# Hybrid layer on one core: the recurrent part's keys turned by TensorE instead of stored twice, the second norm's weights spread by TensorE instead of loaded

## The reference, cut to what matters

```python
h = rms_norm(x, norm1_w); proj = h @ w_in
# 8 heads of stick-breaking attention (width 64), 4 heads of gated delta net (width 128)
gq, gk, gv = split(silu(causal_conv(gdn_qkv)));  gq, gk = l2_normalize(gq) * 128**-0.5, l2_normalize(gk)
x = x + concat(rms_norm(attention), rms_norm(gated_delta_net(gq, gk, gv, ...)) * gate) @ w_out
x = x + peer_ffn(rms_norm(x, norm2_w))
# peer_ffn: per token 8 heads x 16 experts of 16384, chosen by top-k over sums of two key scores;
#   act = gelu(u_table[expert] . xb) * gate;  out = sum(act * v_table[expert])
```

## Time and profile before

| | |
|---|---|
| median of 3 runs | 3555.86 us (3548.87 to 3561.72) |
| the profiled execution, its own time | 3561.24 us |
| its span, first to last instruction | 3559.5 us |
| busy: PE, DVE, POOL, ACT | 66%, 65%, 65%, 24% |
| bytes moved | 1276.24 MB, mean 359 GB/s |
| of these the gathers (software queue) | 1073.87 MB |

### The profile page before, as it was taken

How to read it: one execution, slowest core, us unless ns; L and a number is a source line. 1 busy time by engine, 2 the same in 40 slices (tenths; PEclk the granted TensorE clock), 3 DMA queues, 4 the chain that set the end, 5 groups by cost and what they waited for, 6 DMA issues and landing times.

```text
span 3559.5 us, 46354 instructions
## 1 busy us (share of the span) xinstructions
PE 2354.7 (66%) x16193; PEld 1425.5 (40%) x16193; DVE 2318.2 (65%) x5421; ACT 849.8 (24%) x2344; POOL 2308.0 (65%) x2091
## 2 busy tenths in 40 slices
PE   7663546885847759767848859758847784344477
PEld 6543424653524436534524536534514451000011
DVE  3436887776697597666698587667696658444400
ACT  3330012331213223313114123314103311111122
POOL 1001775555667777677777677577687768777775
PEclk9887657897868879878869879878858885555555
DMA  7542899998989999999999999999999999999999
GB/s 233 190 169 97 312 356 328 351 374 301 349 321 357 410 373 411 412 381 390 409 374 387 409 384 410 368 389 395 406 371 369 407 409 346 387 409 409 409 403 374
DMA packets 398905, 1276.24 MB, mean 359 GB/s; under 512 B 44302, under 2 KB 99667, under 8 KB 389459
## 3 DMA queue, kind: packets, MB, share of 16 engines
q0 software_dynamic: 294912, 1073.87, 78.2%
q1 hardware_dynamic: 85330, 157.45, 12.2%
q10 hardware_dynamic: 18432, 41.95, 3.2%
HBM read 1232.18 MB, written 40.93 MB: 358 GB/s over the span
## 4 chain that ended last, share of the span: by engine, by line
POOL 25%; PE 24%; DVE 18%; DMA 17%; issue 9%; ACT 3%; DVEq 3%; ACTq 1%; SPq 0%; POOLq 0%
PE zz L1489 14%; POOL u_ring L684 13%; POOL v_ring L699 11%; DMA v_ring<-in_peer_v,idxT 9%; DVE u_ring L1067 5%; PE va L1489 4%; PE rr L1489 4%; DMA u_ring<-in_peer_u,idx 4%; DMA u_ring<-in_peer_v,idxT 2%; PE ox L1489 1%; DMA work<-d_w 1%; POOL u_ring L699 1%; DVE work L1398 1%; DVE work L1400 1%; DMA work<-d_gv 1%
## 5 line engine op out<-in xcount | busy, mean ns | idle before, releaser
L684 POOL DMA_INDIRECT u_ring<-in_peer_u,idx x1024 | 1177.2, 1150 | 786.4 <-DVE work L1414 330.3
L1067 DVE SCALAR_TENSOR_TENSOR u_ring<-u_ring,hn_t 128x1024 f32<-128x1024 f32 x1024 | 1223.1, 1222 | 387.2 <-DMA u_ring<-in_peer_u,idx 383.6
L699 POOL DMA_INDIRECT v_ring<-in_peer_v,idxT x960 | 1061.5, 1106 | 422.2 <-issue 248.6
L1489 PE MATMUL va<-v_ring,column 128*32 128x256 f32 x7680 | 748.3, 493 | 618.3 <-DMA v_ring<-in_peer_v,idxT 562.8
L1489 PE MATMUL zz<-work 128*128 128x256 f32 (+3 forms) x3232 | 739.0, 390 | 62.4 <-DVE work L1248 12.6
L1489 PEld LDWEIGHTS zz<-work 128*128 128x128 f32 (+1 forms) x3232 | 552.6, 212 | 270.7 <-issue 136.6
L1489 PEld LDWEIGHTS va<-v_ring,column 128*32 128x32 f32 x7680 | 196.9, 124 | 1096.9 <-DMA v_ring<-in_peer_v,idxT 888.0
L763 ACT ACTIVATE column<-onehot,wT 128x32 f32<-128x32 f32 x1024 | 285.9, 315 | 805.7 <-PE va L1489 777.5
L1489 PE MATMUL zz<-work,w_q_t 128*128 128x128 f32 x1024 | 132.0, 292 | 1.8 <-DVE work L1314 1.8
L1489 PEld LDWEIGHTS zz<-work,w_q_t 128*128 128x128 f32 x1024 | 127.1, 206 | 14.2 <-issue 11.5
L1489 PE MATMUL rr<-work,later 128*128 128x512 f32 x144 | 97.3, 796 | 40.0 <-DVE work L1267 31.1
(11 more groups left out here) (245 smaller groups left out, 2519.1 us busy)
## 6 DMA issues: line engine op xcount, KB each, us to landing
work<-d_w SPq DMA_DIRECT2D x42, 1024.0 KB, 8.5
work<-in_w_out ACTq DMA_DIRECT2D x64, 512.0 KB, 9.5
u_ring<-in_peer_u,idx POOLq DMA_INDIRECT x1024
v_ring<-in_peer_v,idxT POOLq DMA_INDIRECT x960, 10.4
work<-d_kT SPq DMA_DIRECT2D x36, 256.0 KB, 8.2
work<-d_v SPq DMA_DIRECT2D x36, 256.0 KB, 6.6
work<-in_x SPq DMA_DIRECT2D x16, 512.0 KB, 7.6
w_q_t<-in_peer_w_q SPq DMA_DIRECT2D x1, 8192.0 KB, 26.6
```

The costliest lines, as they stand in the source:

```text
L684: g.indirect_dma_start(u_ring[:, n % RU, :], None, u_rows, bass.IndirectOffsetOnAxis(idx[b % 2][:, s:s + 1], 0)).then_inc(u_landed[n % RU] ...
L699: g.indirect_dma_start(v_row(n), None, v_rows, bass.IndirectOffsetOnAxis(idxT[b % 3][:, t:t + 1], 0)).then_inc(v_landed[slot] if slot < RV ...
L1067: v.scalar_tensor_tensor(u_ring[:, m % RU, :], u_ring[:, m % RU, :], 1.0, hn_t[b % 2][:, :], ALU.mult, ALU.mult, accum_out=dots[:, s:s + 1 ...
L1489: return t_.matmul(out_, lhsT, rhs, start=start, stop=stop, skip_group_check=True)
```

## The change

1. `needs_tokens` holds for the value chunks alone. The scratch tensor `d_gk`, its 16 stores and its 8 loads are gone. In the first "start" step of a block TensorE transposes `gkT` (four heads) into the bank `ox` 1, ahead of the products of pairs, and ScalarE copies it to `gk`; VectorE waits for that copy ahead of L1204. The later transpose in the same bank counts on the same semaphore and waits for that copy.
2. The 8 loads of `norm2_w` over all partitions are gone. After `out_done` ScalarE makes 8 diagonal matrices of 128 x 128 (`ident` scaled by a column of weights) in the tile where the loaded weights stood, ahead of its wait for `h_turned`. After the transposes of the sum TensorE multiplies a matrix of ones with each, which writes the weights, repeated over all partitions, into `ox`; VectorE's L1322 reads them from there.
3. `ox` bank 1 is no longer free at point "hn", and TensorE waits for `hn_done` before the point after the first query group. With fewer transposes in the projections, their steps 19 to 21 and 26, 27 count as having a free bank. Worked through `table()`, one thing moves: TURN of block 4 goes from point 242 (step 28) to 240 (step 26), and the use of that block's first 5 v tiles from point 243 to 241. The u tiles of every point stay.

```diff
 def needs_tokens(n):
-    return CH[n][0] == "v" or (CH[n][0] == "g" and CH[n][1] >= GH)
+    return CH[n][0] == "v"
...
-                                          ("key", b + 1, 9.0, 1), ("mix", 1, 8.0, 1), ("out", 2, 10.0, 1), ("hn", 1, 8.0, 1),
+                                          ("key", b + 1, 9.0, 1), ("mix", 1, 8.0, 1), ("out", 2, 10.0, 1), ("hn", 1, 8.0, None),
...
-        norm2b = T(W + 4, 2)
+        n2_diag = heads(T(W + 4, 2), KC)
...
-                for dst, src in ((ab_in[:, :], d_ab), (gkT, d_gkT), (gqT, d_gqT), (gk, d_gk), (gv, d_gv)):
+                for dst, src in ((ab_in[:, :], d_ab), (gkT, d_gkT), (gqT, d_gqT), (gv, d_gv)):
...
-                sp.dma_start(norm2b, norm2_w[0:1, :].to_broadcast([P, D])).then_inc(n2_landed, 16)
...
                 a.activation(t_qd, bank(zz, 0), ACT.Exp).then_inc(qd_exp, 1)
+                act.wait_ge(start_turned, 2 * b + 1)
+                a.activation(gk, bank(ox, 1), ACT.Copy).then_inc(start_copied, 1)
...
-                act.wait_ge(h_turned, b + 1)
+                act.wait_ge(out_done, b + 1)
+                for k in range(KC):
+                    last = a.activation(n2_diag[:, k, :], ident[:, :], ACT.Copy, scale=vecs[:, R_N2 + k:R_N2 + k + 1])
+                last.then_inc(n2_ready, 1)
+                act.wait_ge(h_turned, 2 * b + 1)
...
+                dve.wait_ge(start_copied, 2 * b + 1)
                 v.tensor_tensor(heads(t_kd, 4), heads(gk, 4), spread(ex[:, 4:8], 4, P), ALU.mult)
...
-                dve.wait_ge(n2_landed, 16 * (b + 1))
-                v.scalar_tensor_tensor(mix, h_sb, rh, norm2b, ALU.mult, ALU.mult).then_inc(hn_done, 1)
+                dve.wait_ge(h_turned, 2 * b + 2)
+                v.scalar_tensor_tensor(mix, h_sb, rh, ox[:, :], ALU.mult, ALU.mult).then_inc(hn_done, 1)
...
                 mm(bank(zz, 1), ones[:, :], t_p).then_inc(spread_done, 1)
+                turn(bank(ox, 1), gkT, GH).then_inc(start_turned, 1)
                 four(bank(rr, 0), gkT, gkT)
                 four(bank(rr, 1), gkT, gqT).then_inc(pairs_done, 1)
...
                 turn(rr[:, :], h_sb, KC).then_inc(h_turned, 1)
+                pe.wait_ge(n2_ready, b + 1)
+                weights_read()
+                for k in range(KC):
+                    last = mm(heads(bank(ox, k // 4), 4)[:, k % 4, :], ones[:, :], n2_diag[:, k, :])
+                last.then_inc(h_turned, 1)
                 at("hn", 0)
...
+                    if q == 0:
+                        pe.wait_ge(hn_done, b + 1)
                     at("pq", q)
```

More of the change, by code:

```diff
@@ L217, in hybrid_layer_kernel @@
     d_gkT = scratch("d_gkT", (NB, P, GH, P))
-    d_gk = scratch("d_gk", (NB, P, GH, P))
     d_gv = scratch("d_gv", (NB, P, GH, P))
@@ L402, in hybrid_layer_kernel @@
         t_corr_done, tt_ready = sem("t_corr_done"), sem("tt_ready")
-        tt_turned, tt_copied = sem("tt_turned"), sem("tt_copied")
+        start_turned, start_copied = sem("start_turned"), sem("start_copied")
         uw_done, uw_copied = sem("uw_done"), sem("uw_copied")
@@ L420, in hybrid_layer_kernel @@
         mix_turned, mixT_act, mixT_dve, out_done = sem("mix_turned"), sem("mixT_act"), sem("mixT_dve"), sem("out_done")
-        xb_landed, n2_landed = sem("xb_landed"), sem("n2_landed")
+        xb_landed, n2_ready = sem("xb_landed"), sem("n2_ready")
         h_done, h_stored, h_squared, h_meaned, h_seeded = (sem("h_done"), sem("h_stored"), sem("h_squared"),
@@ L511, in projection @@
                         t = token_count(m) - 1
-                        dst = d_gv if CH[m][0] == "v" else d_gk
                         sp.wait_ge(turned_copied, TOKS * g + t + 1)
-                        sp.dma_start(dst[b0:b0 + SEG, :, CH[m][1] % 4, :].rearrange("b t c -> t b c"),
+                        sp.dma_start(d_gv[b0:b0 + SEG, :, CH[m][1] % 4, :].rearrange("b t c -> t b c"),
                                      tok_ring[t % 2].rearrange("p (b c) -> p b c", b=SEG)).then_inc(tok_stored[t % 2], 16)
@@ L889, in mixing @@
                 a.activation(t_dt, t_dt, ACT.Exp).then_inc(decay_exp, 1)
-                act.wait_ge(tt_turned, b + 1)
-                a.activation(t_T, bank(ox, 1), ACT.Copy).then_inc(tt_copied, 1)
+                act.wait_ge(start_turned, 2 * b + 2)
+                a.activation(t_T, bank(ox, 1), ACT.Copy).then_inc(start_copied, 1)
                 at("start", 2)
@@ L1181, in mixing @@
                 g_next = segment_before(b + 1) if b + 1 < NB else None
-                dve.wait_ge(gdn_landed, 80 * (b + 1))
+                dve.wait_ge(gdn_landed, 64 * (b + 1))
                 v.tensor_copy(g_sel[0:64, 0:4], ab_in[0:64, 0:4])
@@ L1232, in mixing @@
                         else:
-                            dve.wait_ge(tt_turned, b + 1)
+                            dve.wait_ge(start_turned, 2 * b + 2)
                         level(lv + 1)
@@ L1312, in mixing @@
                 v.tensor_tensor(h_sb, zz[:, :], x_in, ALU.add).then_inc(h_done, 1)
-                dve.wait_ge(h_turned, b + 1)
+                dve.wait_ge(h_turned, 2 * b + 1)
                 v.tensor_copy(hT[:, 512:1024], bank(rr, 1)).then_inc(hT_dve, 1)
@@ L1593, in mixing @@
                 pe.wait_ge(tt_first, b + 1)
-                turn(bank(ox, 1), t_TT, 4).then_inc(tt_turned, 1)
+                pe.wait_ge(start_copied, 2 * b + 1)
+                turn(bank(ox, 1), t_TT, 4).then_inc(start_turned, 1)
                 at("start", 2)
@@ L1598, in mixing @@
                     if lv == 1:
-                        pe.wait_ge(tt_copied, b + 1)
+                        pe.wait_ge(start_copied, 2 * b + 2)
                     else:
```

## The result

| | us | ratio to before, same chip | 95% interval |
|---|---|---|---|
| before | 3555.16 (3548.87 to 3561.72, 5 runs) | | |
| after | 3506.44 (3502.39 to 3511.68, 5 runs) | 0.9861 | 0.9844 to 0.9878 |

The change makes the kernel 48.7 us faster, 1.4%. I had forecast 28 us, and a range that began at 3508. The sign was right. The size was not, since I had priced the largest part of the gain, the steps of projections 1 to 3, at 4 us, and had given nearly half of the forecast to bytes, which turned out to count for little.

A forecast was written before the change was run, and what follows sets the result against it. It took the main chain as the bound before the first gather, partly until 1157 us, then DMA. Terms -8 -1 -4 -2.5 +2 -11 -4 = -28.5 us gave a median of 3528 us (-0.8%), range 3508 to 3549.

The forecast's parts named there:

- What bounds the kernel: Main chain at full price before the first gather, partly up to 1157 us, then only DMA time, one gap excepted.
- The sign that I had named: A check on the DMA-bound reading: after 1157 us the DMA share stays at 1.00 or above.
- Projections 2 and 3: Projection steps there: DMA is full, so removing key transposes and their waits gains nothing.
- Projection(1): Projection steps with DMA partly unused: a faster chain can be fed, 4 us gained, between 0 and 10.6.
- Projection(0): Projection steps ahead of the first gather: key transposes and their waits go, 8 us gained, at most 10.6.
- DMA work removed: 8.39 MB fewer stores and loads: 11 us gained after 1157 us, 2.5 us from 340 to 1157 us.
- The gap at 2288: End of projection(3): GpSimd's 18.18 us wait for a v slot shortens by the earlier turn, 4 us gained.
- The norm's weights: Diagonals and products replacing the loads: ScalarE nearly covered, TensorE about 1 us per block, 2 us lost in all.
- the transfers were hidden: Rival: the chain of mixings sets the end and nothing in it gets shorter; -6 us, 3550 us, chance 0.18.
- The case of all ceilings: Rival: projections 0 and 1, load, DMA and gap all reach their ceilings, 46.8 us, 3509 us, chance 0.14.
- The slower case: Rival: the mixing chain sets the end with TensorE's additions on it in every block; +15 us, 3571, chance 0.06.
- The limit of 358 GB/s: Skill's effective HBM rate per core; as the bound, 8.39 MB would be worth 23.4 us wherever they lie.

The follow-up runs named there:

- e15: Kernel before with ScalarE's copies of transposed tiles moved to the start of its step in projections 2 and 3 alone: 3794.03 us, 0.9952, slower chip.
- e3: Kernel after with key transposes, their copies and the old turn of block 4's weights back, no key stores or loads: 3545.67 us, 0.9983 to before.
- e2: Kernel before with the norm's part of the change alone, keys still stored and loaded twice: 3551.12 us, 0.9996 to before.
- e4: Kernel after with the 16 key stores to HBM back, without transposes, copies or loads: 3507.16 us, 0.9883 to before.
- e12: Kernel after with the turn of block 4's weights at step 28 again, nothing else: 3506.53 us, 0.9878 to before.
- e9: Kernel after, unchanged, run again on another chip for comparison: 3506.37 us, 0.9885 to before.
- e16: Kernel after with the 8 loads of norm2_w put back into a free tile, unused: 3765.93 us, 0.9871 to before, slower chip.
- e11: Kernel after with 16.8 MB of unused copies from HBM to HBM added on SP's queue: 3533.21 us, 0.9946 to before.
- e5: Kernel before with ScalarE's copies of transposed tiles moved to the start of its step, all else kept: 0.9898 to before, slower chip.
- e8: Kernel after with 16.8 MB of unused copies from HBM to HBM added, on a slower chip: 0.9894 to before.
- e13: Kernel before with ScalarE's copies of transposed tiles at the start of its step in all projections, run again: 3770.82 us, 0.9902, slower chip.
- e18: Kernel after, unchanged, run on a slower chip beside before with ScalarE's copy first: 3739.33 us, 0.9891 to before.

## Why the prediction was wrong in size, step by step

- **What bounds the kernel: wrong.** "In that region two thirds of the run is set by the 16 DMA engines" is the step that failed. A share of 1.02 did not mean that a shorter main chain would find no room. GpSimd waited 162 us for slots after 1157 us, and slots are freed by VectorE and TensorE at points of the main chain. e15 shows it: with all bytes kept and the share at 0.98 to 1.02 in those stretches, the move in projections 2 and 3 saves 8 to 28 us. Two readings had misled me. The 888 us of the earlier trace rows are those of the weight loads, which wait beside running products; TensorE's products themselves waited 562.8 us for v tiles. And I had taken 1.03 for "full" from the stretch after 3044 us; there GpSimd is itself busy for 256.1 of 336 us, and has 77.4 us of gaps between issues and 2.8 us of slot waits, so that its own pace may set the 405 GB/s as well as the DMA engines. No run separates the two. TensorE's own row, before, whole run:

```profile
PE va L1489 <- DMA v_ring<-in_peer_v,idxT: 562.8, 389, 5.7
```

The sign that I had named for my reading (a share of 1.00 or above after 1157 us) came out and yet said nothing for it: the share rose from 1.01 to 1.02 while a shorter chain gave the time.
- **Projections 2 and 3, "nothing": wrong.** The stretches became 7 and 12 us shorter, where I had only 4 us for the gap and some 2 to 4 us of bytes. With the waits back and no bytes (e3) they are 223 and 211 us again, all of the first and half of the second.
- **Projection(1), 4 us: mis-sized.** Its stretch became 13 us shorter, more than my ceiling of 10.6; the waits for the copies fell there from 14.6 to 3.3 us. The DMA share rose from 0.94 to 0.98, so part of the room that I had seen was used. I had taken little more than a third of the ceiling, with no number behind that choice.
- **Projection(0), 8 us: right in kind and nearly in size.** The waits of the earlier trace rows for key tiles are gone; the waits for copies in this projection fell from 13.1 to 3.3 us. Two of the four transposes that are left stand late, the second with 1.66 us of waiting. In order of time on TensorE, after:

```profile
130.27 0.38 PE L1498 MATMUL ox<-ident,work 128*128 128x128 f32 x2
136.19 0.41 PE L1498 MATMUL ox<-ident,work 128*128 128x128 f32 x2 [1.66 <-ACT work L860]
```

Block 0 began 9.3 us earlier, load included (forecast 9), and the first gather 7.1 us earlier. This pair of traces understates the gain. GpSimd's wait for the first indices is 330.3 to 333.7 us in the four traces that keep all the waits of projection(0) (before, e2, e3, e15), and 316.4 to 323.8 us in all others. Part of that spread is not the change's: after, e4 and e12 begin block 0 at 163.5 us with a mean granted clock of 0.91 in the first 40 us, e9 at 158.1 us with 0.96. Among traces with 0.91 there (e2, e3, e15 against after, e4, e12), block 0 begins 10.5 to 12 us earlier and that wait is 10 us shorter. The rows are those of VectorE's first copy and of the gathers in after:

```profile
163.48 0.16 DVE L1187 COPY sm<-ab_in 64x4 f32<-64x4 f32 x1 [4.94 <-DMA work<-d_gv]
```

```profile
L682 POOL DMA_INDIRECT u_ring<-in_peer_u,idx x1024: 933/938/2087, 333.3 to 3312.8; - x171
```

- **DMA work removed, 13.5 us: mis-sized.** e3, which moves none of the 8.4 MB, is 1 to 10 us under before. e4 (2.1 MB) and e16 (4.2 MB) show nothing, e2 nothing for 4.2 MB with the products added. Where bytes were seen at all (e11), they cost 1.3 to 1.6 us per MB, by which the 4.7 MB after 1157 us would be some 7 us. With these intervals the term can't be split further.
- **The gap at 2288, 4 us from the moved turn: not seen in the time.** The longest wait for a v slot in projection(3) fell from 18.2 us to 1.7, as I had said (under 10). In e12, with the turn back at its old step and the key transposes gone, it is 9.9 us. So about half of the gap came from the waits in front of the turn and half from its place, and the second half is worth nothing that can be measured: e12 equals after.
- **The norm's weights: hidden as forecast, one price off.** Around the sum of block 1, after:

```profile
936.31 2.45 ACT L953 ACTIVATE work<-ident,vecs 128x128 f32<-128x128 f32 x8 [16.83 <-PE zz L1494]
936.38 1.23 DVE L1317 TENSOR_TENSOR work<-zz,work 128x1024 f32<-128x1024 f32 x1 [10.11 <-PE zz L1494]
937.66 1.09 PE L1498 MATMUL rr<-ident,work 128*128 128x128 f32 x8 [0.39 <-DVE work L1317]
938.79 0.60 ACT L956 ACTIVATE work<-rr 128x512 f32<-128x512 f32 x1
938.81 2.05 PE L1494 MATMUL ox<-work,ones 128*128 128x128 f32 x16
942.37 1.28 DVE L1327 SCALAR_TENSOR_TENSOR hn_t<-work,sm,ox 128x1024 f32<-128x1024 f32 x1
```

The diagonals end at 938.76 and L956 starts at 938.79, 0.04 us after the transposes: covered. The spread weights end at 940.9, 1.5 us ahead of L1327: covered. But 8 products are 16 rows of TensorE, 2.05 us at full clock and not 1.0; I had taken two rows of one float32 product for two products. It stayed unseen in the time, as e2 shows no loss.
- **The rivals.** That the transfers were hidden and the chain of mixings sets the end was the better half of the truth: bytes were nearly hidden, but in that chain something did get shorter, the projections, which I had priced there at next to nothing. With the rival's own reading of the bound and 10 us for each of four projections, the forecast would have been 40 us, 3516. The case of all ceilings came nearest in number (3509), by the wrong sum. The slower case was out: TensorE's additions cost nothing measurable.
- **The rules of the Trainium skill.** The limit of 358 GB/s (Trainium skill, HBM Reference, "Specifications") would have made all removed bytes count, 23.4 us; e3's 1 to 10 us for all of them speak against it, and so does e11, where 16.8 MB cost 27 us and not 47. Overheads of small DMAs (Trainium skill, Perfetto Trace Analysis, "DMA Optimizations") were not seen in time: with the rows of 512 B back, e4 takes 3507.16 us, within the noise of after.

## What to carry to other kernels

Where one engine issues all gathers in order, add up its own line (busy, issue gaps, waits for slots) before calling a kernel DMA-bound. Slot waits at a full DMA share are a reason to doubt it, and no proof: here 162 us of them lay there and a shorter chain did pay, but e11's bytes lengthened them as well. The test is to shorten one wait without touching a byte. In a pipeline written by steps, look for a hand-over that ends one engine's step and begins the other's: with a single buffer the two run in turn. Here moving the copy to the front of its step added no work and gave most of the gain. Take out bytes and waits in separate runs: here the part that removed waits and 4.2 MB gave 1.1%, the part that removed 4.2 MB and no such wait 0.0%.

## What the runs showed that I had not expected

- A DMA share of 1.02 and 400 GB/s over 222 us did not keep projection(2) from taking 7 us less, also with its key stores kept (e4).
- 16.8 MB of added copies cost 26.8 us on one chip, and nothing visible on another, where every kernel took 7% longer and the last stretch gathered at 365 GB/s:

```profile
3200.00:3500.00 300.00, 123.24 (x852) 29.74 (x844) 131.26 (x214) 31.98 (x107) 219.36 (x209) 0.52 0.97 366
```

In all ten traces of those chips (e5 to e8, e13 to e18) GpSimd waits 109 to 145 us for a slot whose releaser reads "remote" in the view of waits; no trace of the faster chips has such a row. Why the chips differ was not tried.
- A float32 product of 128 x 128 x 128 shows as two rows of TensorE.
